# Router logits with the weights held still, and the work between LayerNorm and the first expert gather in another order

## The chip, the cores and the metric

The kernel runs on one core of one Trainium2 chip. The metric is the device time of one execution in microseconds (us). TensorE (PE; its weight loads are listed as PEld) multiplies, VectorE (DVE) and ScalarE (ACT) do elementwise work, GpSimd (POOL) and SyncE (SP) mostly issue DMAs here. TensorE writes into PSUM, eight banks of 128 partitions x 512 float32 numbers; everything else lies in SBUF.

## The reference

Two layers over 304 tokens (272 of a prompt, 32 of a sample). Layer 0 mixes tokens by gated linear attention and latent attention, layer 1 by pooling; each ends in `x = layer_norm(ALPHA * x + out)` and is followed by a mixture of experts and another LayerNorm:

```python
scores = sigmoid(x2 @ router_w)                       # 1024 x 64
biased = scores + router_b
group_score = sum(top_k(biased in 8 groups of 8, 2))  # best 4 groups
idx = top_k(biased inside those groups, 8)
wts = scores[idx] / sum(scores[idx]) * 2.5
routed = sum over idx of wts * (silu(x @ w_gate[e]) * (x @ w_up[e])) @ w_down[e]
shared = (silu(x2 @ sh_gate) * (x2 @ sh_up)) @ sh_down
return layer_norm(ALPHA * x + routed + shared)
```

There are 64 experts with a hidden width of 256; all arithmetic is float32.

## The kernel before

Tokens lie in three tiles of 128, 128 and 64 rows (`ROWS`; 320 columns `T_COLS`, padded to 384). `x` is token-major, `xt` its transpose, eight slices of 128 rows. Each engine runs its own program; semaphores join them. PSUM banks are given out in turn by a fixed list, `bank_uses()` (L211): opening a name waits until the bank's earlier user has been copied out.

Between a mixer and the experts of layer `l` TensorE runs (L1123 to L1150): transposes of x (`xT`, five parts: two for each full tile, one for the last), router products (`lg`, L1130: for each tile, eight products with 128 tokens as weights and the 64 router columns moving), the shared expert's gate and up products (`sg`, `su`, two halves b each, L1134), slot positions (`pos`, L1140: triangular and all-ones matrices times the 0/1 selection), the shared down products (`sd`, L1149), and then `pe_experts` (L756), which reads the number of rounds into a register and gathers the tokens of the first eight experts (L814: eight gathers of five products into banks 2 and 3 in turn). One float32 product is two TensorE instructions; those of the gather (fp32r) are one.

ScalarE makes the LayerNorm's 1/sqrt (`ln_rsqrt`, L1218) for all three tiles, copies `xT` parts 0, 2, 4 into xt (`copy_xt`), takes exp of the logits, makes `xh`, the rounded high part of x (L1346, L1347), and the Silu of sg (L1350). VectorE copies `xT` parts 1 and 3, computes the selection (L1673 to L1705), the normed weights and their split in two parts (L1707 to L1716), the masked selection that `pos` reads (L1717), `sh_h` = Silu(sg) * su (L1723), the slots and the number of rounds (L1724 to L1738), the low parts `xl` of x (L1742, L1743), in layer 0 two identity blocks of `spread` (L1748), the six additions of the shared output to x (L1755), and in `dve_experts` its register load, the weights into `spread` and the one-hot matrix `pick` of the first group (L1364, L1365). Gathered tokens are copied by ScalarE (even slices) and VectorE (odd ones) in turn.

The expert loop then runs over 32 pairs of experts. SyncE (`sp_experts`) loads their weights into two slots; the shared weights lie in the second slot, so its loads wait for `su` and `sd`. In this data one round is enough.

## Time and profile before

| | us |
|---|---|
| median of 3 runs | 1543.93 (1543.57 to 1546.67) |
| profiled execution, its own time | 1544.77 |
| its span in the trace | 1543.0 |
| PE busy | 1454.6 (94%) |
| VectorE busy | 648.0 (42%) |
| ScalarE busy | 364.0 (24%) |

The chain that ended last is TensorE for 90% of the span. All times in the rows below are counted from the span's start. A timeline row has start, duration, engine, line, operation, output <- inputs, the partition and column tile for TensorE, shapes and the number of instructions merged; behind it in brackets the idle time before it and what ended that. In a table of stretches the clock is TensorE's granted clock, 1.00 for 2.4 GHz and 0.50 for 1.2 GHz.

### The profile page before, as it was taken

To read this page: it belongs to the slowest core of one execution; us is meant where nothing else is said; L and a number is where in the kernel's file an instruction comes from. 1 tells how busy PE (TensorE), PEld (TensorE's weight loads), DVE (VectorE), ACT (ScalarE), POOL (GpSimd) and SP (SyncE) were. 2 spreads that over 40 slices of the span, in tenths; PEclk is the share of its full clock that TensorE was granted. 3 is DMA by queue.
4 is the path that set the end of the run, shared out by engine and by line. 5 is a ranking of instruction groups with operands and counts; after the bars stand their busy time and mean duration, and the time that the engine had idled before them with its cause. 6 is when DMAs were issued, how large, how long until landed. Compare 5 with 4: busy or idle time off the path is not lost.

```text
span 1543.0 us, 17906 instructions
## 1 busy us (share of the span) xinstructions
PE 1454.6 (94%) x6555; PEld 772.0 (50%) x6555; DVE 648.0 (42%) x1290; ACT 364.0 (24%) x726; POOL 45.4 (3%) x76
## 2 busy tenths in 40 slices
PE   6998999879999999999999878799999999999995
PEld 4564555555444454454454466454454454444542
DVE  0654532463334334343333466533343343433336
ACT  1441321312122122121221243021221221221213
POOL 4200100100000000000000010000000000000000
PEclk9996557799999999999999986999999999999998
DMA  9102110455998999899899822289989989998970
GB/s 290 64 1 110 42 54 0 160 195 206 391 376 350 420 382 391 367 396 391 350 410 395 346 81 82 109 347 393 374 367 412 374 350 423 379 393 365 394 325 31
DMA packets 63623, 435.31 MB, mean 282 GB/s; under 512 B 4324, under 2 KB 6436, under 8 KB 13537
## 3 DMA queue, kind: packets, MB, share of 16 engines
q1 hardware_dynamic: 60800, 427.18, 69.1%
q0 software_dynamic: 2784, 7.62, 1.7%
q8 instruction: 24, 0.39, 0.1%
q14 instruction: 15, 0.12, 0.0%
HBM read 433.02 MB, written 1.76 MB: 282 GB/s over the span
## 4 chain that ended last, share of the span: by engine, by line
PE 90%; DVE 7%; issue 1%; DMA 1%; ACT 0%; POOL 0%; SPq 0%; DVEq 0%
PE bank L832 29%; PE bank L753 26%; PE bank L786 14%; PE bank L780 12%; PE bank L737 4%; PE bank L842 1%; PE bank L902 1%; DVE sb_ln_st L1444 1%; DVE sb_x L1451 1%; DVE sb_x L1454 1%; PE bank L1008 1%; PE bank L1005 1%; PE bank L1001 1%; DVE sb_x L1755 1%; DVE sb_xl L1423 1%
## 5 line engine op out<-in xcount | busy, mean ns | idle before, releaser
L1378 DVE TENSOR_TENSOR sb_x<-sb_x,bank 128x512 f32<-128x512 f32 (+1 forms) x396 | 242.2, 680 | 118.6 <-PE bank L780 118.6
L786 PE MATMUL bank<-sb_wslot,sb_ht 128*64 128x512 f32 x1024 | 231.0, 593 | 0.0
L832 PE MATMUL bank<-sb_wslot,sb_xg_own 128*64 128x512 f32 x1024 | 226.5, 595 | 1.9 <-DVE sb_xg_own L1370 1.9
L832 PE MATMUL bank<-sb_wslot,sb_xt 128*64 128x512 f32 x1024 | 226.8, 595 | 0.0
L1400 DVE TENSOR_TENSOR sb_hh<-sb_sg,bank 128x256 f32<-128x256 f32 x64 | 27.0, 421 | 367.5 <-ACT sb_sg L1186 367.5
L753 PE MATMUL bank<-sb_pick,sb_xh 128*128 128x512 f32 x432 | 162.9, 406 | 15.6 <-DVE sb_pick L1365 15.6
L1384 DVE SCALAR_TENSOR_TENSOR sb_yl<-bank,sb_gslot,sb_yh 128x512 fp32r<-128x512 f32 x128 | 96.1, 751 | 162.8 <-ACT sb_yh L1168 162.8
L780 PE MATMUL bank<-sb_yh,sb_place 128*128 128x512 f32 x396 | 157.5, 398 | 3.3 <-DVE sb_yl L1384 3.3
L780 PE MATMUL bank<-sb_yl,sb_place 128*128 128x512 f32 x396 | 156.6, 396 | 0.0
L1186 ACT ACTIVATE sb_sg<-bank 128x256 f32<-128x256 f32 x64 | 24.6, 384 | 552.5 <-PE bank L832 552.5
L786 PEld LDWEIGHTS bank<-sb_wslot,sb_ht 128*64 128x64 f32 x1024 | 72.8, 137 | 144.5 <-issue 139.3
L832 PEld LDWEIGHTS bank<-sb_wslot,sb_xg_own 128*64 128x64 f32 x1024 | 71.4, 137 | 140.8 <-issue 139.8
L832 PEld LDWEIGHTS bank<-sb_wslot,sb_xt 128*64 128x64 f32 x1024 | 70.7, 137 | 139.5 <-issue 139.5
L1168 ACT ACTIVATE sb_yh<-bank,sb_gslot 128x512 fp32r<-128x512 f32 x128 | 88.2, 689 | 174.2 <-PE bank L786 174.2
L753 PE MATMUL bank<-sb_pick,sb_xl 128*128 128x512 f32 x288 | 115.0, 399 | 0.0
L753 PEld LDWEIGHTS bank<-sb_pick,sb_xh 128*128 128x128 f32 x432 | 82.6, 191 | 34.3 <-issue 17.3
L780 PEld LDWEIGHTS bank<-sb_yh,sb_place 128*128 128x128 f32 x396 | 74.3, 188 | 27.3 <-DVE sb_x L1378 5.8
L780 PEld LDWEIGHTS bank<-sb_yl,sb_place 128*128 128x128 f32 x396 | 74.5, 188 | 17.2
L1162 ACT ACTIVATE sb_xg_own<-bank 128x512 f32<-128x512 f32 x72 | 43.1, 599 | 97.4 <-PE bank L753 97.4
L753 PEld LDWEIGHTS bank<-sb_pick,sb_xl 128*128 128x128 f32 x288 | 55.3, 192 | 10.3
L1162 ACT ACTIVATE sb_xt<-bank 128x512 f32<-128x512 f32 x64 | 38.4, 599 | 37.7 <-PE bank L753 37.7
L737 PEld LDWEIGHTS bank<-sb_cst,sb_hh 128*128 128x128 f32 x128 | 20.7, 205 | 46.0 <-issue 45.4
(295 smaller groups left out, 1265.5 us busy)
## 6 DMA issues: line engine op xcount, KB each, us to landing
sb_wslot<-in_moe_w_gate_dram SPq DMA_DIRECT2D x64, 2048.0 KB, 8.1
sb_wslot<-in_moe_w_up_dram SPq DMA_DIRECT2D x64, 2048.0 KB, 12.8
sb_wslot<-in_moe_w_down_dram SPq DMA_DIRECT2D x64, 2048.0 KB, 15.1
sb_w_in_hi<-in_w_in_dram SPq DMA_DIRECT2D x2, 2048.0 KB, 22.4
sb_w_in_lo<-in_w_out_dram SPq DMA_DIRECT2D x1, 4096.0 KB, 13.4
sb_w_in_lo<-in_w_in_dram SPq DMA_DIRECT2D x2, 1024.0 KB, 10.9
sb_ln_g<-in_ln_g_dram POOLq DMA_DIRECT2D x4, 512.0 KB, 4.7
sb_ln_b<-in_ln_b_dram POOLq DMA_DIRECT2D x4, 512.0 KB, 6.1
```

What stands on the lines that cost most here:

```text
L737: return pe.transpose(dst, src, ident[0:n, 0:n])
L753: last = pe.matmul(dst, lhs, rhs, start=i == 0, stop=i == len(pairs) - 1)
L780: last = pe.matmul(banks.tile[order[f]][:, :], place[u][:, t * P:(t + 1) * P], part[:, c * 512:(c + 1) * 512], start=h == 0, stop=h == 1)
L786: last = pe.matmul(y_b[c][64 * e:64 * e + 64, :], ht[:, k, 64 * e:64 * e + 64], w_down[u][:, e, k * D + c * 512:k * D + (c + 1) * 512], st ...
L832: last = pe.matmul(gu_b[64 * e:64 * e + 64, :], xgt[b][:, k, sl], w_gu[u][:, :, e, k * FE:(k + 1) * FE], start=k == 0, stop=k == DK_SLICES ...
L842: last = pe.matmul(place_b[:, t * PLACED:(t + 1) * PLACED], pick[b][:, t, q * P:(q + 1) * P], spread[:, b, t, :], start=True, stop=True)
L1162: act.activation(xgt[b][:, kk, :], banks.tile[2 + c][:, :], ACT.Copy).then_inc(s[f"xg_copied{c}"], 1)
L1168: act.activation(yh[:, c * 512:(c + 1) * 512], banks.tile[4 + c][:, :], ACT.Copy, scale=gslot[:, u, :]).then_inc(s[f"yh_ready{c}"], 1)
L1186: act.activation(sg[:, :], gu_b[:, 0:FE], ACT.Silu).then_inc(s["sg_ready"], 1)
L1378: dve.tensor_tensor(dst, dst, banks.tile[order[f]][0:rows, :], ALU.add).then_inc(s["added"], 1)
L1384: dve.scalar_tensor_tensor(out=yl[:, cc], in0=banks.tile[4 + c][:, :], scalar=gslot[:, u, :], in1=yh[:, cc].bitcast(F32), op0=ALU.mult, op ...
L1400: dve.tensor_tensor(hh[:, :], sg[:, :], gu_b[:, FE:2 * FE], ALU.mult).then_inc(s["h_ready"], 1)
```

## The change

The router weights become the weights of TensorE, and the tokens move: the first four slices of K are summed on output partitions 0 to 63, the other four on 64 to 127 (bank `lgT`), first for the 256 tokens of two tiles, then, behind the third tile's transposes, for the last 128. ScalarE copies the 64+64 rows x 384 tokens to `lg_t`, and three products with `two_idents` (two identities of 64 on top of each other) add the halves and bring the logits back token-major. ScalarE copies all five `xT` parts of these stages and all eight gathered slices, splits x tile by tile as each is ready, and writes the identities of `spread`. VectorE subtracts tile by tile, compares all tiles in one operation, writes the masked selection into its own tile `chosen`, and does the normed weights only after the additions. `pos` runs ahead of the last `su`, the register load ahead of `sd`, and `pick` ahead of the additions. The gather waits for banks 2 and 3 alone; the loop waits for the rest (`w_ready`). Cut to its core:

```diff
+    def freed(self, eng, b, name):
+
+n = sum(1 for k in range(self.order.index(name) + 1) if k % 8 == b)
+eng.wait_ge(self.emptied[b], n)
...
-u += [("xT", l + 1, i) for i in range(5)]
-u += [("lg", l)] + [(n, l, b) for b in range(2) for n in ("sg", "su")] + [("pos", l)]
+u += [("xT", l + 1, i) for i in range(4)] + [("lgT", l), ("xT", l + 1, 4), ("lg", l)]
+u += [("sg", l, 0), ("su", l, 0), ("sg", l, 1), ("pos", l), ("su", l, 1)]
...
-sc = rb("sc", [P, TILES, E])
+lg_t = rb("lg_t", [P, T_PAD])
...
-cnt = rb("cnt", [P, E])
+sc = rb("sc", [P, TILES, E])
+sel = rb("sel", [P, TILES, E])
+chosen = rb("chosen", [P, TILES, E])
+tmp = rb("tmp", [P, TILES, E])
...
+    shared_down()
+    pe.wait_ge(s["x_split"], TILES)
+    pe.wait_ge(s["xl_ready"], TILES)
     pe.wait_ge(s["pick_ready"], 1)
+    for b in (2, 3):
+        banks.freed(pe, b, ("sd", l, TILES - 1, 1))
     for kk in range(DK_SLICES):
         if kk > 1:
             pe.wait_ge(s[f"xg_copied{kk % 2}"], kk // 2)
         gather(0, kk)
+    banks.all_copied(pe, ("sd", l, TILES - 1, 1))
+    pe.wait_ge(s["init"], 5)
+    pe.wait_ge(s["w_ready"], 2 - l)
...
+        pe_transpose_x(pe, l + 1, range(4))
...
+        both = banks.open(pe, ("lgT", l))
+
+        def logits(cols):
+            for kk in range(4):
+                for h in range(2):
+                    last = pe.matmul(both[64 * h:64 * h + 64, cols], w_rt[:, 4 * h + kk, :], xt[:, 4 * h + kk, cols],
+                                     start=kk == 0, stop=kk == 3)
+            return last
+
+        for i in range(4):
+            banks.copied(pe, ("xT", l + 1, i))
+        logits(slice(0, 2 * P))
+        pe_transpose_x(pe, l + 1, (4,))
+        banks.copied(pe, ("xT", l + 1, 4))
+        logits(slice(2 * P, T_PAD)).then_inc(banks.fill_sem(("lgT", l)), 1)
+        banks.copied(pe, ("lgT", l))
         ps = banks.open(pe, ("lg", l))
         for t in range(TILES):
-            last = accumulate(pe, ps[:, t * E:(t + 1) * E], [(xt[:, k, t * P:(t + 1) * P], w_rt[:, k, :]) for k in range(8)])
+            last = pe.matmul(ps[:, t * E:(t + 1) * E], lg_t[:, t * P:(t + 1) * P], const("two_idents"), start=True, stop=True)
         last.then_inc(banks.fill_sem(("lg", l)), 1)
...
+        def shared(name, w, b):
+            stage((name, l, b), lambda ps: accumulate(pe, ps[:, 0:T_COLS], [
+                (w[:, k, b::2], xt[:, k, 0:T_COLS]) for k in range(8)]))
...
+        shared("sg", sh_gate, 0)
+        shared("su", sh_up, 0)
+        shared("sg", sh_gate, 1)

         pe.wait_ge(s["sel_ready"], 1)
...
+            accumulate(pe, ps[:, t * E:(t + 1) * E], [(const("ones"), chosen[:, i, :]) for i in range(t)] +
...
+        shared("su", sh_up, 1)
+
+        def shared_down():
+            for b in range(2):
+                banks.copied(pe, ("su", l, b))
+            token_products("sd", l, lambda k, tc: sh_h[:, k, tc], sh_down, 2)
+
+        pe_experts(pe, l, shared_down)
...
-    for m in range(QUAD):
-        copy_xg(0, 2 * m, m + 1)
+    for kk in range(DK_SLICES):
+        copy_xg(0, kk, kk // 2 + 1)
...
-    ln_rsqrt(0)
...
+        def split_high(t):
+            rows = ROWS[t]
+            act.wait_ge(x_ready, 6 * l + t + 1)
+            act.activation(xh[0:rows, t, :, :], x[0:rows, t, :].rearrange("p (f k) -> p k f", k=DK_SLICES), ACT.Copy)\
+               .then_inc(s["x_split"], 1)
+
+        ln_rsqrt(2 * l, (0, 1))
+        copy_xt(l + 1, (0, 1))
...
+        split_high(0)
+        ln_rsqrt(2 * l, (2,))
+        copy_xt(l + 1, (2, 3))
+        split_high(1)
+        copy_xt(l + 1, (4,))
+        copy(lg_t[:, :], ("lgT", l), lambda ps: ps[:, 0:T_PAD])
...
-        act.activation(xh[:, 0:2, :, :], by_k(x[:, 0:2, :]), ACT.Copy)
-        act.activation(xh[0:64, 2, :, :], x[0:64, 2, :].rearrange("p (f k) -> p k f", k=DK_SLICES), ACT.Copy)\
-           .then_inc(s["x_split"], 1)
+        split_high(2)
+        if l == 0:
+            act.wait_ge(s["init"], 5)
+            for b in range(2):
+                act.activation(spread[:, b, 0:2, 0:P], bc(ident, 1, 2), ACT.Copy)
+                ins = act.activation(spread[0:64, b, 2, 0:P], ident[0:64, :], ACT.Copy)
+            ins.then_inc(s["w_ready"], 1)
...
-    def copy_xg(b, kk, n):
-        dve.wait_ge(s["xg_done1"], n)
-        dve.tensor_copy(xgt[b][:, kk, :], banks.tile[3][:, :]).then_inc(s["xg_copied1"], 1)
+        spread_weights(b, c0)
+        pick_slots(b, c0)

...
-    pick_group(0, slice(0, GROUP_E))
-    for m in range(QUAD):
-        copy_xg(0, 2 * m + 1, m + 1)
...
-        copy_xt(l + 1)
...
+        def split_low(t):
+            rows = ROWS[t]
+            dst = xh[64:128, 2, :, :] if t == 2 else xl[:, t, :, :]
+            dve.wait_ge(s["x_split"], t + 1)
+            dve.tensor_tensor(dst, x[0:rows, t, :].rearrange("p (f k) -> p k f", k=DK_SLICES),
+                              xh[0:rows, t, :, :].bitcast(F32), ALU.subtract).then_inc(s["xl_ready"], 1)
+
+        def spread_weights(b, c0):
+            return dve.tensor_copy(spread[:, b, :, P:].rearrange("p t (e h) -> p t e h", h=2), w_split[:, :, c0, :])
+
+        def pick_slots(b, c0):
+            iota = bc(bc(const("iota"), 1, GROUP_E), 1, TILES)
+            dve.tensor_tensor(pick[b][:, :, :].rearrange("p t (e n) -> p t e n", e=GROUP_E), iota,
+                              bc(pos_x[:, :, c0], 3, SLOTS), ALU.is_equal).then_inc(s["pick_ready"], 1)
+
+        split_low(0)
+        split_low(1)
...
-        for t in range(TILES):
-            other, own = bc(gs[:, t, :], 1, NG), bc(gs[:, t, :], 2, NG)
-            tt(cmp1[:, t, :, :], other, own, ALU.is_gt)
-            tt(cmp2[:, t, :, :], other, own, ALU.is_equal)
-            tt(cmp2[:, t, :, :], cmp2[:, t, :, :], const("lower_group").rearrange("p (g n) -> p g n", g=NG), ALU.mult)
+        other, own = bc(gs[:, :, :], 2, NG), bc(gs[:, :, :], 3, NG)
+        lower = bc(const("lower_group").rearrange("p (g n) -> p g n", g=NG), 1, TILES)
+        tt(cmp1[:, :, :, :], other, own, ALU.is_gt)
+        tt(cmp2[:, :, :, :], other, own, ALU.is_equal)
+        tt(cmp2[:, :, :, :], cmp2[:, :, :, :], lower, ALU.mult)
...
-        tt(tmp[:, :, :], sc[:, :, :], sel[:, :, :], ALU.mult)
-        step(dve.tensor_reduce(wsum[:, :], tmp[:, :, :], AX.X, ALU.add))
...
-        tt(sel[:, :, :], sel[:, :, :], valid, ALU.mult, s["sel_ready"])
...
+        tt(chosen[:, :, :], sel[:, :, :], valid, ALU.mult, s["sel_ready"])
+
+        def gate_hidden(b):
...
             dve.tensor_tensor(sh_h[:, b, :], sh_sg[:, b, :], ps[:, 0:T_COLS], ALU.mult).then_inc(banks.empty_sem(n), 1)
+
+        gate_hidden(0)
+        split_low(2)
...
-        dve.wait_ge(s["x_split"], 1)
-        for t in range(2):
...
-           ALU.subtract, s["x_split"])
...
-            dve.wait_ge(s["init"], 5)
-            for b in range(2):
-                step(dve.tensor_copy(spread[:, b, 0:2, 0:P], bc(ident, 1, 2)))
-                step(dve.tensor_copy(spread[0:64, b, 2, 0:P], ident[0:64, :]))
+        gate_hidden(1)
+        pick_slots(0, slice(0, GROUP_E))
...
-        dve_experts(dve, l, step)
+        tt(tmp[:, :, :], sc[:, :, :], sel[:, :, :], ALU.mult)
+        step(dve.tensor_reduce(wsum[:, :], tmp[:, :, :], AX.X, ALU.add))
...
+        step(dve.tensor_copy(w_split[:, :, E:, :], w_split[:, :, 0:GROUP_E, :]))
+        if l == 0:
+            dve.wait_ge(s["init"], 5)
+        spread_weights(0, slice(0, GROUP_E)).then_inc(s["w_ready"], 1)
+        dve_experts(dve, l, spread_weights, pick_slots)
```

## Rows read from the trace of the kernel before

**Rows 1.** Page, part 2: TensorE's busy tenths in 40 slices of 38.6 us.

```profile
PE   6998999879999999999999878799999999999995
```

**Rows 2.** TensorE's longest waits, 355:905 (us, times, longest); then one stretch of the loop.

```profile
PE bank L780 <- DVE sb_yl L1384: 1.7, 1, 1.7
...
387.00:404.00 17.00, 17.00 (x79) 8.13 (x77) 5.82 (x11) 3.62 (x7) 0.00 (x0) 1.00 0.96 386
```

**Rows 3.** Timeline, layer 0, TensorE: start us, us, engine, line, operation [idle before].

```profile
291.71 1.14 PE L737 MATMUL bank<-sb_cst,sb_x 64*128 64x64 f32 x8 [0.66 <-DVE sb_x L1454]
293.95 10.48 PE L753 MATMUL bank<-sb_w_rt,sb_xt 128*128 128x64 f32 x48 [1.10 <-POOL sb_yl L723]
304.22 19.57 PE L753 MATMUL bank<-sb_xt,sb_wslot 128*128 128x320 f32 x64
...
325.58 7.08 PE L753 MATMUL bank<-sb_wslot,sb_xg_own 128*128 128x512 f32 x16
...
343.04 0.76 PE L753 MATMUL bank<-sb_pick,sb_xh 128*128 128x512 f32 x1 [8.50 <-DVE sb_pick L1365]
...
354.95 7.09 PE L832 MATMUL bank<-sb_wslot,sb_xg_own 128*64 128x512 f32 x32 [0.98 <-DVE sb_xg_own L1370]
```

**Rows 4.** The same timeline in layer 1.

```profile
937.42 10.47 PE L753 MATMUL bank<-sb_w_rt,sb_xt 128*128 128x64 f32 x48 [1.10 <-ACT sb_xt L1207]
947.69 18.70 PE L753 MATMUL bank<-sb_xt,sb_wslot 128*128 128x320 f32 x64
...
984.24 0.77 PE L753 MATMUL bank<-sb_pick,sb_xh 128*128 128x512 f32 x1 [7.11 <-DVE sb_pick L1365]
```

**Rows 5.** Stretches: us, busy (x) of PE, PEld, DVE, ACT, POOL, clock, DMA, GB/s.

```profile
243.40:247.50 4.10, 4.10 (x17) 1.67 (x16) 1.97 (x5) 0.00 (x0) 0.00 (x0) 0.55 0.00 0
248.00:276.00 28.00, 27.52 (x64) 12.08 (x64) 3.75 (x7) 1.78 (x3) 0.00 (x0) 1.00 0.00 1
304.20:308.50 4.30, 4.30 (x10) 2.83 (x10) 3.21 (x9) 3.95 (x2) 0.00 (x0) 0.50 1.01 426
345.70:354.00 8.30, 8.27 (x35) 6.33 (x33) 2.08 (x3) 2.24 (x4) 0.00 (x0) 0.98 0.00 0
984.30:987.50 3.20, 3.20 (x8) 2.52 (x9) 0.00 (x0) 0.60 (x1) 0.00 (x0) 0.50 0.00 0
```

**Rows 6.** Timeline, mixer stage: TensorE's pairs on 64 output columns each.

```profile
68.59 3.67 PE L926 MATMUL bank<-sb_w_in_hi,sb_xt 128*64 128x256 f32 x32
...
243.36 4.19 PE L1084 MATMUL bank<-sb_w_in_hi,sb_w_uv 128*64 128x320 f32 x16
```

**Rows 7.** Timeline, layer 0, ScalarE.

```profile
286.47 1.28 ACT L1215 ACT_TABLE_LOAD   x1 [4.60 <-DVE sb_ln_mv L1445]
...
292.89 0.60 ACT L1207 ACTIVATE sb_xt<-bank 128x512 f32<-128x512 f32 x1 [2.05 <-PE bank L737]
...
304.77 3.92 ACT L1346 ACTIVATE sb_xh<-sb_x 128x2048 fp32r<-128x2048 f32 x1
```

**Rows 8.** Timeline, layer 0, VectorE.

```profile
305.01 0.26 DVE L1426 TENSOR_SCALAR sb_sc<-sb_sc 128x192 f32<-128x192 f32 x1 [12.03 <-ACT sb_sc L1344]
...
316.31 0.36 DVE L1423 TENSOR_TENSOR sb_tmp<-sb_sc,sb_sel 128x192 f32<-128x192 f32 x1
...
319.31 0.36 DVE L1423 TENSOR_TENSOR sb_sel<-sb_sel,sb_cst 128x192 f32<-128x192 f32 x1
...
323.83 0.49 DVE L1723 TENSOR_TENSOR sb_xg_own<-sb_xg_own,bank 128x320 f32<-128x320 f32 x1 [3.64 <-PE bank L753]
325.78 0.36 DVE L1727 TENSOR_SCALAR sb_pos_x<-bank 128x192 f32<-128x192 f32 x1 [1.47 <-PE bank L753]
...
328.49 4.07 DVE L1423 TENSOR_TENSOR sb_xl<-sb_x,sb_xh 128x1024 fp32r<-128x1024 f32 x2
...
341.04 0.19 DVE L1364 CAST sb_spread<-sb_w_split 128x48 fp32r<-128x48 f32 x1 [0.96 <-DVE sb_x L1755]
341.15 1.74 DVE L1365 TENSOR_TENSOR sb_pick<-sb_cst,sb_pos_x 128x1536 fp32r<-128x1536 f32 x1
```

More of the change, by code:

```diff
@@ L107, in constants @@
     put(cst, CST, "lower_group", np.tile((g[None, :] < g[:, None]).reshape(1, -1), (P, 1)))
+    put(cst, CST, "two_idents", np.tile(np.eye(E), (2, 1)))
     mix = np.zeros((P, MIX_W), f)
@@ L444, in build @@
         mr = rb("mr", [P, TILES, E])
-        sel = rb("sel", [P, TILES, E])
-        tmp = rb("tmp", [P, TILES, E])
         mx8 = rb("mx8", [P, TILES, 8])
@@ L737, in transpose, with pe_transpose_x @@
             return pe.transpose(dst, src, ident[0:n, 0:n])
-        def pe_transpose_x(pe, n):
-            for i in range(5):
+        def pe_transpose_x(pe, n, parts):
+            for i in parts:
                 t, k0, nk = xt_part(i)
@@ L759, in pe_experts @@
             xg_b, y_b = banks.tile[2:4], banks.tile[4:6]
-            banks.all_copied(pe, ("sd", l, TILES - 1, 1))
             def gather(b, kk):
@@ L868, in _ @@
             pe.wait_ge(x_in, 16 * 5)
-            pe_transpose_x(pe, 0)
+            pe_transpose_x(pe, 0, range(5))
             def stage(name, pairs_of):
@@ L1141, in _ @@
                 for t in range(TILES):
-                    accumulate(pe, ps[:, t * E:(t + 1) * E], [(const("ones"), sel[:, i, :]) for i in range(t)] +
-                               [(const("before"), sel[:, t, :])])
-                accumulate(pe, ps[:, TILES * E:(TILES + 1) * E], [(const("ones"), sel[:, i, :]) for i in range(TILES)])\
+                    accumulate(pe, ps[:, t * E:(t + 1) * E], [(const("ones"), chosen[:, i, :]) for i in range(t)] +
+                               [(const("before"), chosen[:, t, :])])
+                accumulate(pe, ps[:, TILES * E:(TILES + 1) * E], [(const("ones"), chosen[:, i, :]) for i in range(TILES)])\
                     .then_inc(banks.fill_sem(("pos", l)), 1)
-                for b in range(2):
-                    banks.copied(pe, ("su", l, b))
-                token_products("sd", l, lambda k, tc: sh_h[:, k, tc], sh_down, 2)
-                pe_experts(pe, l)
+                shared("su", sh_up, 1)
[4 more added lines that the diff above has]
+                pe_experts(pe, l, shared_down)
         def act_experts(act, l):
@@ L1207, in copy, with copy_xt @@
                 act.activation(dst, src(ps) if src else ps, ACT.Copy).then_inc(banks.empty_sem(name), 1)
-            def copy_xt(n):
-                for i in range(0, 5, 2):
+            def copy_xt(n, parts):
+                for i in parts:
                     t, k0, nk = xt_part(i)
@@ L1216, in rsqrt, with ln_rsqrt @@
                 step(act.activation(dst, dst, ACT.Exp, scale=-0.5), sem)
-            def ln_rsqrt(n):
-                for t in range(TILES):
+            def ln_rsqrt(n, tiles=range(TILES)):
+                for t in tiles:
                     rows = ROWS[t]
@@ L1222, in ln_rsqrt @@
                     rsqrt(ln_rs[0:rows, t:t + 1], ln_mv[0:rows, t, 1:2], 1.0, eps[0:rows, 0:1], rs_ready)
-            copy_xt(0)
+            copy_xt(0, range(0, 5, 2))
             for j in range(2, 4):
@@ L1353, in _, with dve_experts @@
                 ln_rsqrt(2 * l + 1)
-        def dve_experts(dve, l, step):
+        def dve_experts(dve, l, spread_weights, pick_slots):
             s = L[l]
@@ L1687, in _ @@
                 tt(gs[:, :, :], g_a[:, :, :, 0], g_b[:, :, :, 0], ALU.add)
-                for t in range(TILES):
-                    other, own = bc(gs[:, t, :], 1, NG), bc(gs[:, t, :], 2, NG)
-                    tt(cmp1[:, t, :, :], other, own, ALU.is_gt)
-                    tt(cmp2[:, t, :, :], other, own, ALU.is_equal)
-                    tt(cmp2[:, t, :, :], cmp2[:, t, :, :], const("lower_group").rearrange("p (g n) -> p g n", g=NG), ALU.mult)
+                other, own = bc(gs[:, :, :], 2, NG), bc(gs[:, :, :], 3, NG)
[3 more added lines that the diff above has]
+                tt(cmp2[:, :, :, :], cmp2[:, :, :, :], lower, ALU.mult)
                 tt(cmp1[:, :, :, :], cmp1[:, :, :, :], cmp2[:, :, :, :], ALU.add)
@@ L1728, in _ @@
                 step.banked(dve.tensor_copy(cnt[:, :], ps[:, TILES * E:(TILES + 1) * E]), banks, n)
-                tt(pos_x[:, :, 0:E], pos_x[:, :, 0:E], sel[:, :, :], ALU.mult)
+                tt(pos_x[:, :, 0:E], pos_x[:, :, 0:E], chosen[:, :, :], ALU.mult)
                 ts(pos_x[:, :, 0:E], pos_x[:, :, 0:E], -1.0, None, ALU.add)
@@ L1738, in _ @@
                 ts(n_rounds[:, :], cmax[:, :], 1.0, None, ALU.add, None, s["rounds_ready"])
-                dve.wait_ge(s["x_split"], 1)
-                for t in range(2):
-                    tt(xl[:, t, :, :], x[:, t, :].rearrange("p (f k) -> p k f", k=DK_SLICES), xh[:, t, :, :].bitcast(F32), ALU.subtract)
-                tt(xh[64:128, 2, :, :], x[0:64, 2, :].rearrange("p (f k) -> p k f", k=DK_SLICES), xh[0:64, 2, :, :].bitcast(F32),
-                   ALU.subtract, s["x_split"])
-                if l == 0:
-                    dve.wait_ge(s["init"], 5)
-                    for b in range(2):
-                        step(dve.tensor_copy(spread[:, b, 0:2, 0:P], bc(ident, 1, 2)))
-                        step(dve.tensor_copy(spread[0:64, b, 2, 0:P], ident[0:64, :]))
+                gate_hidden(1)
+                pick_slots(0, slice(0, GROUP_E))
                 for t in range(TILES):
```

36 lines of the change are left out of this document (10 added, 26 removed).

## Prediction

> **What bounds the kernel now.** I read the page's slices first: TensorE is busy nine tenths or more nearly throughout, with dips in slices 8 and 9 and again in 23 to 26 [rows 1]. Each expert loop is TensorE's own. In the list of TensorE's waits from 355 to 905 us the loop's own longest is 1.7 us, for yl, and none is for a DMA; a stretch of 17 us shows 17.00 us busy at a clock share of 1.00 while the DMAs moved 386 GB/s [rows 2]. So a microsecond saved before a loop should shift the whole loop. The two routing stretches, where the dips are, I read as a timeline of TensorE: 289 to 355 us in layer 0 [rows 3] and 937 to 984 us in layer 1 [rows 4]. Three losses are to be seen. The router's products take 10.48 us as 48 instructions of 64 columns, each with 128 columns of weights, 0.218 us apiece. TensorE idles 8.50 us (layer 1: 7.11) between the shared down products and the first gather. And it pays for low clock after each: 1.2 instead of 2.4 GHz, share 0.50, for the first 4.3 us of the shared products and the first 3.2 us of layer 1's gather [rows 5].
>
> **Router products.** Of 24 logical products of 128 token weights, 16 become ones that hold 64 router columns and stream 256 or 128 tokens, two halves of K at once on two column halves; then three fold the halves by a doubled identity. What TensorE does with such pairs is in two rows: 32 instructions of 256 columns in 3.67 us at full clock (0.115 each), 16 of 320 columns in 4.19 us at low clock (0.262 each, half of what 320 columns cost alone) [rows 6]. At low clock 16 instructions of 256 columns then take 16 x 0.262 x 256/320 = 3.4 us. No pair of 128 columns is in the trace; it lies between that rate (1.7 us) and the present 0.218 per load (3.5 us); I take 1.7, since a load is now 64 columns, not 128. The fold's six instructions are like the present ones: 6 x 0.218 = 1.3.
> In layer 0 the second tile's transposes end 0.66 before 291.71 [rows 3]; its ACT copies (0.60 each, row 292.89 [rows 7]) end near 291.8, and TensorE follows 0.4 later, as 0.46 separates today's last copy and 293.95. From 292.2: 3.4, the third tile's transposes 1.14, hand-over and copy 1.1, second part 1.7, hand-over and copy of lg_t 1.0, fold 1.3. That is 301.9, against 304.22: 2.3 us saved. Layer 1 has the same spacing; 2.4.
> ACT takes over all five xt copies and the splits. An x tile costs 1.96 us (half of 3.92) [rows 7]. split_high(0) sits ahead of the third tile's rsqrt, which starts today at 286.47; copies from about 283.8 and the split end at 287.1, so rsqrt ends 0.6 us later, about when VectorE asks. I count 0, at most 0.6. split_high(1) (291.8 to 293.8) is over before the third tile's bank fills at 296.8: cost 0. If TensorE's first part were as short as 1 us, it would be in the way.
>
> **Selection.** From the first operation on sc at 305.01 to the end of sel at 316.31 are 11.3 us; `chosen` adds 0.4 [rows 8]. The nine comparisons of a tile each become three larger ones, which only shortens this. Cover is now three shared stages, 48 instructions of 0.27 us (0.43 for 512 columns, 27.52 us for 64, times 320/512 [rows 5]), 13.0 us at full clock. The chain starts 0.5 behind the fold and needs at most 11.7, so slack is 0.8 us or more. The two split_low ahead of it (2.03 each, half of 4.07 [rows 8]) run from 291.7 to about 296, before the logits exist. The ten weight operations (3.0 us, 316.31 to 319.31) leave this chain for the time behind the adds, under the gather of 9.4 us: cost 0, and what passes 9 us there would be exposed before the loop.
>
> **Order of pos and su.** pos now comes ahead of the last shared stage, so the slot chain (325.78 to 328.49, 2.7 us [rows 8]) runs under 4.3 us of products. The price: the shared down products now wait directly for the last su, its multiplication and two hand-overs, near 0.9 us, where today pos lies between. TensorE's load of the number of rounds stands there too; VectorE's such load shows as 0.96 idle before 341.04 [rows 8]. In parallel it costs nothing, behind the wait another 1.0. Bounds 0.9 to 1.9; I take 1.4 in each layer.
>
> **The gap before the gather.** Today VectorE does after n_rounds: 4.07 of split, 2.0 more, the identity casts (layer 0), six adds, the register load, 0.19 and 1.74 for slots, ending at 342.9 [rows 8]. After, splits are done early, casts go to ACT (behind sc, before the first Silu, nobody waits), and pick_slots (1.74) begins some 0.5 us after the last su, 9 us before the shared down products end. By the bank order those of tile 0 take banks 2 and 3, which the gather needs; they are added 5 us before it. So the whole gap goes: 8.5 and 7.1 us. What is late next is TensorE itself. The gather then follows dense work and runs at full clock: 40 instructions x 0.236 (8.27 us for 35 [rows 5]) = 9.4 instead of 10.9 (343.04 to 353.97), 1.5 saved; layer 1, with 3.2 us at low clock, 1.6. Now all eight copies are ACT's, 0.6 every 1.17 us: no wait; the last is 0.1 shorter than VectorE's.
>
> **Clock in the shared products.** They took 19.57 and 18.70 us; 64 x 0.27 is 17.3. In the present trace the clock stayed at 1.2 GHz through all of the router's 10.48 us and rose 4.3 us into the dense products behind them [rows 5]. After the change 3.4 us of dense pair products come before. The 4.1 us of pair products at 243.4 show a share of 0.55, and the 512-column ones right behind them 1.00 [rows 5]. I take it as full when the shared products begin: 2.2 and 1.4 saved. If it is not, these fall away (+3.6); if it is full from the second part of the logits on, another 1.9 per layer goes.
>
> **Sum.** Layer 0: -2.3 + 1.4 - 8.5 - 1.5 - 0.1 - 2.2 = -13.2. Layer 1: -2.4 + 1.4 - 7.1 - 1.6 - 0.1 - 1.4 = -11.2. Together -24.4 from the profiled execution's own 1544.8: 1520.4. The median of the runs lies 0.8 lower, so **1519.6 us**. With the clock late 1523.2, with it early 1515.8; hand-overs and 128-column loads add 1.0 and 3.6 at most.
> SP's order is untouched. The load of the second slot's gate, issued behind the shared down products, has 10 us less lead before the first expert pair, but serves the second pair, 16 us later.
>
> **Rivals.**
> *The halves run one after the other.* Both halves use all 128 rows, and their weights might not load beside the other's product. Then the logits cost 3.4 + 1.7 us more in each layer: 1519.6 + 10.2 = 1529.8. The pair rows speak against it [rows 6]. The Trainium skill ("TensorE: Matmul & The Clock Gate", Part 3, "The mechanism") says that a weight load overlaps a product in flight only when their row groups differ, which is not so here; by that rule the time would be this rival's. The trace disagrees: pairs on all 128 rows came every 0.115 us for 256 columns. Chance 4%.
> *VectorE or ACT becomes the bound.* If the selection is late by 2 us (slack 0.8) or pick_slots and hand-overs are, TensorE waits and part of the clock is lost: +3 us a layer, 1525.6. For it: ten small links in a row. Against it: slack at each, as above. Chance 15%.
> *The gain is swallowed by the weights.* If the loop ran at the DMAs' pace, an earlier start would move nothing: 1544. Against it, no wait of TensorE on a DMA [rows 2]. Chance 2%.
> *Slower: the clock does not come back.* The place is from the fold to the end of the gather. The logits now have four short stops of TensorE. If these kept it at 1.2 GHz through shared, pos, down and gather (17.3 + 2.1 + 9.0 + 9.4 = 37.8 us at full clock), each layer pays 37.8 in place of what I saved as clock (3.7 and 3.0): 1519.6 + 75.6 + 6.7 = 1602. It decides from about 12 us of low-clock work extra per layer, so a return later than 24 us after the first shared product. Against it: the clock rose within 4.3 us each time dense work began [rows 5]. Chance 3%.
>
> **Chances.** Forecast with its clock variants (1514 to 1524) 76%, late selection 15%, serial halves 4%, swallowed 2%, slower 3%. The range 1513 to 1528 takes in the variants and late selection, without the last three. A measurement here tells about 0.2%, 3 us, from no change. Faster 0.95, same 0.02, slower 0.03.
>
> **What would show it.** Logits as 32 + 6 instructions from transposes to the first shared product in under 11 us; no idle over 1 us between shared down and gather; gather at 0.234 us an instruction from its first; first expert product 13 and then 24 us earlier. TensorE waiting for `chosen`, or an expert loop longer than before, would make the prediction wrong.

## The result, and the profile after

The changed kernel takes 1519.28 us (median of 4 runs, 1516.69 to 1521.64), the kernel before 1544.4 beside it. The ratio is 0.9831, 95% interval 0.9817 to 0.9844. The forecast was 1519.6. The profiled execution has a span of 1519.9 us.

TensorE's timeline in layer 0 is to be laid beside [rows 3]; columns are as there.

```profile
291.22 1.97 PE L746 MATMUL bank<-sb_cst,sb_x 128*128 128x128 f32 x8 [4.80 <-DVE sb_x L1494]
293.96 3.47 PE L1145 MATMUL bank<-sb_xt,sb_w_rt 128*64 128x256 f32 x16 [0.78 <-ACT sb_xt L1242]
297.36 1.09 PE L746 MATMUL bank<-sb_cst,sb_x 64*128 64x64 f32 x8
299.14 1.09 PE L1145 MATMUL bank<-sb_xt,sb_w_rt 128*64 128x128 f32 x16 [0.69 <-ACT sb_xt L1242]
300.83 0.88 PE L1158 MATMUL bank<-sb_cst,sb_lg_t 128*128 128x64 f32 x6 [0.59 <-ACT sb_lg_t L1242]
301.55 13.14 PE L762 MATMUL bank<-sb_xt,sb_wslot 128*128 128x320 f32 x48
314.53 2.12 PE L762 MATMUL bank<-sb_chosen,sb_cst 128*128 128x64 f32 x18
316.48 4.53 PE L762 MATMUL bank<-sb_xt,sb_wslot 128*128 128x320 f32 x16
321.69 7.10 PE L762 MATMUL bank<-sb_wslot,sb_xg_own 128*128 128x512 f32 x16 [0.68 <-issue]
328.73 1.94 PE L903 MATMUL bank<-sb_wslot,sb_xg_own 128*64 128x512 f32 x8
330.60 0.50 PE L762 MATMUL bank<-sb_pick,sb_xh 128*128 128x512 f32 x1
```

Four things are to be seen. The router's products are now the two L1145 rows and the fold (L1158), 38 instructions instead of 48. `pos` (314.53) stands inside the shared stages. The first gather (330.60) starts behind the last shared down product with no idle time in its bracket, where [rows 3] has 8.50. And its first product takes 0.50 us, not 0.76: the clock is up. In layer 1 the same rows are:

```profile
922.81 3.68 PE L1145 MATMUL bank<-sb_xt,sb_w_rt 128*64 128x256 f32 x16 [0.78 <-ACT sb_xt L1242]
926.43 1.14 PE L746 MATMUL bank<-sb_cst,sb_x 64*128 64x64 f32 x8
928.25 1.98 PE L1145 MATMUL bank<-sb_xt,sb_w_rt 128*64 128x128 f32 x16 [0.69 <-ACT sb_xt L1242]
930.82 1.54 PE L1158 MATMUL bank<-sb_cst,sb_lg_t 128*128 128x64 f32 x6 [0.59 <-ACT sb_lg_t L1242]
932.15 14.74 PE L762 MATMUL bank<-sb_xt,sb_wslot 128*128 128x320 f32 x48
...
953.90 7.11 PE L762 MATMUL bank<-sb_wslot,sb_xg_own 128*128 128x512 f32 x16 [0.68 <-issue]
...
973.26 7.09 PE L846 MATMUL bank<-sb_wslot,sb_xg_own 128*64 128x512 f32 x32 [0.87 <-ACT sb_xg_own L1197]
```

The second part of the logits takes 1.98 us here and 1.09 in layer 0, the fold 1.54 and 0.88. That is the granted clock, 1.00 in layer 0's second part and 0.50 in layer 1 from both parts of the logits until 3 us into the shared products. In the changed kernel's table of stretches, with columns as in [rows 5], the clock is the third figure from the end of a row:

```profile
293.90:297.40 3.50, 3.44 (x17) 1.98 (x17) 3.50 (x2) 1.91 (x1) 3.50 (x6) 0.55 0.72 220
299.10:300.20 1.10, 1.06 (x16) 0.85 (x16) 0.00 (x0) 0.00 (x0) 0.00 (x0) 1.00 1.04 432
922.80:926.40 3.60, 3.59 (x16) 1.90 (x16) 3.60 (x2) 1.83 (x1) 1.05 (x2) 0.50 0.61 146
932.10:935.20 3.10, 3.10 (x8) 2.12 (x8) 2.23 (x4) 2.78 (x3) 0.00 (x0) 0.50 0.00 0
935.20:946.00 10.80, 10.80 (x41) 7.79 (x41) 9.73 (x32) 1.21 (x2) 0.00 (x0) 0.99 0.00 0
```

The starts of the same instructions in the timelines of all profiles cut the execution into stretches, in us. They are: (a) first transposes to first shared product, (b) to the first shared down product, (c) to the gather, (d) to the first expert product. For before, layer 0, they are 283.14 (the transposes of tile 0), then the starts in [rows 3].

| kernel | start to (a) | layer 0: a, b, c, d | loop | LayerNorm, pooling | layer 1: a, b, c, d | rest |
|---|---|---|---|---|---|---|
| before | 283.1 | 21.08, 21.36, 17.46, 11.91 | 530.6 | 40.0 | 22.13, 20.49, 16.06, 12.12 | 546.6 |
| changed | 285.3 | 16.29, 20.14, 8.91, 10.48 | 530.7 | 41.3 | 19.09, 21.75, 8.90, 10.46 | 546.6 |

Layer 0's four fell from 71.81 to 55.82, by 16.0 us, layer 1's from 70.80 to 60.20, by 10.6. The loops did not move. The two parts that the change does not touch were 2.1 and 1.3 us longer in this one execution. Of the 2.1, 1.8 are in the kernel's first projections, the same 64 instructions in 19.28 us here and 17.46 before. Over the 14 profiles of this study the start varied from 280.4 to 285.3 and the pooling stretch from 39.7 to 43.3. So 26.6 less 3.5 (2.1, 1.3 and 0.1 in the loop) are the 23.1 us between the two spans.

### The profile page after: what moved, and what is told of

Its sections match the earlier page's. It is cut to its first block, busy times and chain, and to the rows that moved or that the text cites. A ratio compares the mean times of both kernels' runs of the same rounds, so it can differ in the third digit from the quotient of the medians.

```text
span 1519.9 us, 17857 instructions
## 1 busy us (share of the span) xinstructions
PE 1445.7 (95%) x6535; PEld 759.0 (50%) x6535; DVE 637.1 (42%) x1262; ACT 372.6 (25%) x746; POOL 45.4 (3%) x76
## 4 chain that ended last, share of the span: by engine, by line
PE 93%; DVE 5%; issue 1%; ACT 1%; DMA 1%; SPq 0%; DVEq 0%
PE bank L846 29%; PE bank L762 25%; PE bank L794 15%; PE bank L788 12%; PE bank L746 4%; PE bank L856 1%; PE bank L916 1%; DVE sb_ln_st L1484 1%; PE bank L1022 1%; PE bank L903 1%; DVE sb_x L1491 1%; DVE sb_x L1494 1%; PE bank L1145 1%; PE bank L1019 1%; PE bank L1015 1%
## 5 line engine op out<-in xcount | busy, mean ns | idle before, releaser
L1197 ACT ACTIVATE sb_xg_own<-bank 128x512 f32<-128x512 f32 x80 | 47.9, 599 | 78.3 <-PE bank L762 78.3
```

The costliest lines, as they stand in the source:

```text
L1197: act.activation(xgt[b][:, kk, :], banks.tile[2 + c][:, :], ACT.Copy).then_inc(s[f"xg_copied{c}"], 1)
```

## The experiments

All are edits of the changed kernel but the first; the diffs are cut. Times are medians, with the ratio to the kernel before on the same chip.

**1. The router products alone, in the kernel before.**

```diff
-pe_transpose_x(pe, l + 1)
+pe_transpose_x(pe, l + 1, range(4))
...
+both = banks.open(pe, ("lgT", l))
...
+logits(slice(0, 2 * P))
+pe_transpose_x(pe, l + 1, (4,))
...
+logits(slice(2 * P, T_PAD)).then_inc(banks.fill_sem(("lgT", l)), 1)
...
 for t in range(TILES):
-    last = accumulate(pe, ps[:, t * E:(t + 1) * E], [(xt[:, k, t * P:(t + 1) * P], w_rt[:, k, :]) for k in range(8)])
+    last = pe.matmul(ps[:, t * E:(t + 1) * E], lg_t[:, t * P:(t + 1) * P], const("two_idents"), start=True, stop=True)
```

> The kernel before with the router products of the change alone (logits through lgT and lg_t; everything else in the old order). My theory: the two traces give a stretch from the first transposes to the first shared product that is 4.8 us shorter in layer 0 (21.08 to 16.29) and 3.0 in layer 1 (22.13 to 19.09), and nothing behind it in the old order is waiting for something else, so about 1537 us, 7 to 8 below the kernel before. Rival: in the old order VectorE's chain, not TensorE, sets the gather's start, and the saving turns into a longer idle before the gather (over 11 us instead of 8.5), so 1544.

1542.73 us, 0.9981 (0.9968 to 0.9993). The stretches: a, b, c, d are 17.90, 19.24, 17.46, 12.63 and 18.83, 20.94, 16.07, 12.37, together 7.2 us under before. Stretch (c) is unchanged at 17.46, so the idle ahead of the gather did not grow and the rival falls. Stretch (a) fell by 3.2 and 3.3 where I had 4.8 and 3.0; in layer 0 another 2.1 came in (b), and (d) took 0.7 and 0.3 more. Of the whole, where I had 7 to 8, only 3.0 us of the medians are seen; in its profile 3.2 us went to the LayerNorm and pooling stretch (43.2), which the edit leaves alone. The profiles of late_pick, late_split_pick and pos_last below have 43.0 to 43.3 there too, so that stretch is not this kernel's own; why the median of ten runs keeps only 3.0 is open.

TensorE's timeline of router_only, the two parts of the logits in layer 0:

```profile
293.14 3.68 PE L1133 MATMUL bank<-sb_xt,sb_w_rt 128*64 128x256 f32 x16 [2.07 <-POOL sb_yh L725]
...
298.58 1.09 PE L1133 MATMUL bank<-sb_xt,sb_w_rt 128*64 128x128 f32 x16 [0.69 <-ACT sb_xt L1223]
```

The first row waits 2.07 us, in the changed kernel 0.78: in the old order VectorE copies two of the transposed parts, and only behind its LayerNorm. The copies on ScalarE are worth 1.3 us a layer to the new router products.

**2. The old router products in the changed kernel.**

```diff
-pe_transpose_x(pe, l + 1, range(4))
+pe_transpose_x(pe, l + 1, range(5))
...
-logits(slice(0, 2 * P))
...
-last = pe.matmul(ps[:, t * E:(t + 1) * E], lg_t[:, t * P:(t + 1) * P], const("two_idents"), start=True, stop=True)
+last = accumulate(pe, ps[:, t * E:(t + 1) * E], [(xt[:, k, t * P:(t + 1) * P], w_rt[:, k, :]) for k in range(8)])
```

> The changed kernel with the old router products (24 products with tokens as weights, after all five transposes). My theory: it loses what the new ones gave, 7 to 8 us: about 1527. The low clock comes back into the first 2 to 4 us of the shared products. Rival, by which most of the gain comes from the later clock and the router products themselves give little: 1521 to 1523.

1532.95 us, 0.9911 (0.9883 to 0.9939), worse than I expected by 6. The eight stretches sum to 127.95 against 116.02, 11.9 more: 5.5 and 3.7 in (a), 1.8 and 1.0 in (b), nothing in (c) and (d).

TensorE's timeline of router_undone, the router's products and the first shared ones in layer 0:

```profile
295.73 10.48 PE L762 MATMUL bank<-sb_w_rt,sb_xt 128*128 128x64 f32 x48 [1.79 <-ACT sb_xt L1228]
306.00 14.89 PE L762 MATMUL bank<-sb_xt,sb_wslot 128*128 128x320 f32 x48
```

The products are the 10.48 us of [rows 3]. They wait 1.79 us, not 1.10, since ScalarE now has the second tile's split (292.67 to 294.77) ahead of the last copy. The edit also takes out ScalarE's copy to `lg_t`. So the two halves of the change help each other: router alone -7.2, the rest alone -14.7, both -26.6. Of the 4.7 between, the rows give 2.6 to the earlier copies (experiment 1) and 1.4 to this wait. These are single profiles: with the second profile of the changed kernel (experiment 9) both together are -29.8, so this division is good to some 3 us only.

**3 to 5. What closed the gap ahead of the gather.** The late split:

```diff
-split_high(0)
...
-split_high(1)
...
-split_high(2)
+for t in range(TILES):
+    split_high(t)
...
-split_low(0)
-split_low(1)
...
-split_low(2)
...
 gate_hidden(1)
+for t in range(TILES):
+    split_low(t)
+dve.wait_ge(s["xl_ready"], TILES)
 pick_slots(0, slice(0, GROUP_E))
```

> The changed kernel with x split late: ScalarE makes the high parts of all tiles behind the exp, VectorE the low parts (6.1 us) behind the last gating and ahead of the slots. My theory: from the last gating VectorE has 9 us under the shared down products; 6.1 + 1.75 + two additions of 0.7 are 9.3, so the gather starts about 0.5 us later in each layer, 1520.3 us in all. Rival: the early splitting is what closed the gap, so 6.1 us come back per layer, 1531.5.

The late one-hot matrix:

```diff
-pick_slots(0, slice(0, GROUP_E))
 for t in range(TILES):
...
+pick_slots(0, slice(0, GROUP_E))
 tt(tmp[:, :, :], sc[:, :, :], sel[:, :, :], ALU.mult)
```

> The changed kernel with the slots' one-hot matrix made behind the six additions, as before the change. My theory: the additions end 1.6 us after the last shared down product and the matrix takes 1.75, so TensorE idles about 3.5 us in each layer: 1526.3, one or two more if the clock falls in the idle. Rival: the matrix is hidden wherever it stands, 1519.3.

Both at once:

> The changed kernel with x split late and the one-hot matrix behind the additions, both at once. My theory: the 6.1 us of splitting run under the shared down products, and only the last additions and the matrix are behind them, so it is like the late matrix alone: 12.5 us from the first shared down product to the gather, and gather at low clock, about 10 us over the changed kernel. Rival: the two add up, 6.1 us more per layer, 18.6 us in that stretch.

| | us | ratio | (c) by layer | (d) by layer |
|---|---|---|---|---|
| late_split | 1517.84 | 0.983 (0.981 to 0.985) | 9.04, 9.04 | 10.45, 10.44 |
| late_pick | 1530.69 | 0.9904 (0.9887 to 0.992) | 12.48, 12.49 | 11.98, 11.89 |
| late_split_pick | 1534.93, one run | | 12.48, 12.48 | 11.99, 11.92 |

The early splitting is worth 0.13 us a layer in the changed kernel: done late, it runs under the shared down products. The place of the one-hot matrix is worth 3.6 us a layer in (c), and 1.5 in (d), since the gather behind the idle starts at low clock. I had put 3.5 and one or two in all. The two do not add up: with both, (c) is the same.

TensorE's timeline of late_pick, the first product of layer 0's gather with the idle ahead of it:

```profile
331.87 0.47 PE L762 MATMUL bank<-sb_pick,sb_xh 128*128 128x512 f32 x1 [3.51 <-issue]
```

VectorE's timeline of late_split_pick, from the splitting to the one-hot matrix:

```profile
322.83 3.92 DVE L1712 TENSOR_TENSOR sb_xl<-sb_x,sb_xh 128x1024 fp32r<-128x1024 f32 x2
326.78 2.00 DVE L1712 TENSOR_TENSOR sb_xh<-sb_x,sb_xh 64x1024 fp32r<-64x1024 f32 x1
328.82 2.85 DVE L1795 SCALAR_TENSOR_TENSOR sb_x<-sb_x,bank 128x512 f32<-128x512 f32 x4
332.08 1.41 DVE L1795 SCALAR_TENSOR_TENSOR sb_x<-sb_x,bank 64x512 f32<-64x512 f32 x2 [0.41 <-PE bank L903]
333.52 1.76 DVE L1720 TENSOR_TENSOR sb_pick<-sb_cst,sb_pos_x 128x1536 fp32r<-128x1536 f32 x1
```

In VectorE's rows the three subtractions (322.83, 326.78) end before the last shared down product fills its bank; the last two additions (332.08) still have to wait 0.41 for it. Before the change (c) was 17.46. The 5.0 us from there to 12.48 are what VectorE no longer does between the first shared down product and the matrix: the slot chain, 2.7 by [rows 8], the register load, 0.96, and the identity casts, 1.15 (334.63 to 335.79 in the kernel before). Layer 1 has no identity casts, and there the difference is 3.6. That sum is an argument from the rows; no run took these out one at a time. The rows also show that the 0.13 is not what the splits cost before the change. There the 6.1 us of splitting (328.49 to 334.6) stood in the same unbroken chain of VectorE ahead of the additions. Taking them alone out of it would, as an estimate, leave 17.46 - 6.1 = 11.4, less than the 12.48 at which the last additions and the matrix stand, so it would have won the same 5.0. No run tried that. In late_split_pick (a) and (b) of layer 0 were 0.65 and 2.58 longer than in the changed kernel, which the idle does not explain: the second part of the logits took 1.09 us at clock 1.00, the fold behind it 1.54, and the shared products ran at 0.50 until 305 us.

**6 and 7. The place of pos, and of the register load.** pos behind all four shared stages:

```diff
 shared("sg", sh_gate, 1)
+shared("su", sh_up, 1)
 pe.wait_ge(s["sel_ready"], 1)
...
-shared("su", sh_up, 1)
...
 split_low(2)
+gate_hidden(1)
...
-gate_hidden(1)
```

> The changed kernel with the slot positions behind all four shared stages again; the register load still ahead of the shared down products. My theory: the slot chain of VectorE (2.7 us) and the load (0.7 to 1.0) are then no longer under a shared stage, so from the first shared product to the first shared down product it takes about 22.9 us at full clock instead of 20.14, 2.7 more in each layer. Rival: the place of pos is indifferent, because the products wait for the gating either way: 20.1.

The same, and the load behind the shared down products:

```diff
-pe.wait_ge(s["rounds_ready"], 1)
-rounds = pe.value_load(n_rounds[0:1, 0:1], min_val=1, max_val=MAX_ROUNDS)
 shared_down()
+pe.wait_ge(s["rounds_ready"], 1)
+rounds = pe.value_load(n_rounds[0:1, 0:1], min_val=1, max_val=MAX_ROUNDS)
```

> The changed kernel with pos behind all four shared stages and the register load behind the shared down products. My theory: pos covers the gating again, so the first shared down product comes 19.2 us after the first shared product instead of 20.14 (at full clock), 0.9 less per layer, and if TensorE loads the register while products are still queued, 8.9 us later the gather starts as now: 1517.5. Rival: the load can only run when the products are done, 0.7 to 1.0 us of idle ahead of the gather, and nothing is won: 1519.3.

pos_last: one run, 1527.69 us; (b) is 23.15 and 22.95, about 2.9 more than 20.15, as expected, and (c) 10.4 instead of 8.9, because the products behind the stop start at low clock. The timeline of pos_last, VectorE and TensorE in layer 0:

```profile
322.46 0.15 DVE L1465 TENSOR_SCALAR sb_n_rounds<-sb_cmax 128x1 int32<-128x1 f32 x1
322.65 1.76 DVE L1720 TENSOR_TENSOR sb_pick<-sb_cst,sb_pos_x 128x1536 fp32r<-128x1536 f32 x1
...
323.65 2.90 PE L762 MATMUL bank<-sb_wslot,sb_xg_own 128*128 128x512 f32 x3 [3.74 <-issue]
```

VectorE has the number of rounds at 322.61; TensorE's next product starts 1.04 us later. That is the price of the load, with the hand-over to it, where nothing covers it.

pos_load_last: 1512.79 us, 0.9799 (0.978 to 0.9818), 4.7 under what I expected. (b) is 19.25 and 19.24 instead of 20.15, 0.9 less in each layer, (c) 8.88: the load in front of the gather costs nothing.

TensorE's timeline of pos_load_last, from the first shared down product to the gather:

```profile
318.49 7.08 PE L762 MATMUL bank<-sb_wslot,sb_xg_own 128*128 128x512 f32 x16
325.50 1.94 PE L903 MATMUL bank<-sb_wslot,sb_xg_own 128*64 128x512 f32 x8
327.37 0.50 PE L762 MATMUL bank<-sb_pick,sb_xh 128*128 128x512 f32 x1
```

There is no idle in the first row's bracket, where the changed kernel has 0.68 at 321.69. So moving pos ahead of the last shared stage was not a gain in itself: it only makes room for the slot chain that the load, standing ahead of the shared down products, waits for. What the shared down products of the changed kernel wait for is the gating. VectorE's timeline of the changed kernel, layer 0, the number of rounds and the last gating:

```profile
319.20 0.15 DVE L1466 TENSOR_SCALAR sb_n_rounds<-sb_cmax 128x1 int32<-128x1 f32 x1
321.11 0.49 DVE L1770 TENSOR_TENSOR sb_xg_own<-sb_xg_own,bank 128x320 f32<-128x320 f32 x1 [1.75 <-PE bank L762]
```

The number is there at 319.35, over 2 us ahead of TensorE's product at 321.69; the gating ends at 321.60. By these rows moving the load alone would give nothing, and with the load moved the old order of pos is better; the load moved with pos in its new place was not run. The rows show 1.8 us of the difference to the changed kernel; the rest is not in these stretches and is not explained, and the intervals of the two ratios overlap.

**8. The halves of K on one column half.**

```diff
-last = pe.matmul(both[64 * h:64 * h + 64, cols], w_rt[:, 4 * h + kk, :], xt[:, 4 * h + kk, cols],
-                 start=kk == 0, stop=kk == 3)
+last = pe.matmul(both[0:64, cols], w_rt[:, 4 * h + kk, :], xt[:, 4 * h + kk, cols],
+                 start=kk + h == 0, stop=kk + h == 4)
...
-    last = pe.matmul(ps[:, t * E:(t + 1) * E], lg_t[:, t * P:(t + 1) * P], const("two_idents"), start=True, stop=True)
+    last = pe.matmul(ps[:, t * E:(t + 1) * E], lg_t[0:64, t * P:(t + 1) * P], const("two_idents")[0:64, :], start=True, stop=True)
...
-copy(lg_t[:, :], ("lgT", l), lambda ps: ps[:, 0:T_PAD])
+copy(lg_t[0:64, :], ("lgT", l), lambda ps: ps[0:64, 0:T_PAD])
```

> The changed kernel with both halves of K on the same 64 output columns, so that no two products of the logits run side by side. My theory: the 16 instructions of 256 tokens take twice as long, 6.9 us at low clock instead of 3.47, those of 128 tokens 2.1 instead of 1.09 at full clock; from the first transposes to the first shared product 19.5 to 21 us in layer 0 instead of 16.29. Rival, the rule that a weight load is only hidden where the rows differ: the pairs gain nothing and the time stays at 16.3.

One run, 1521.81 us. (a) is 18.83 in layer 0 and 20.71 in layer 1.

TensorE's timeline of one_column, the two parts of the logits in layer 0:

```profile
293.11 5.08 PE L1145 MATMUL bank<-sb_xt,sb_w_rt 128*64 128x256 f32 x16 [0.78 <-ACT sb_xt L1242]
...
299.90 1.96 PE L1145 MATMUL bank<-sb_xt,sb_w_rt 128*64 128x128 f32 x16 [0.69 <-ACT sb_xt L1242]
```

The second part in the table of stretches, columns as in [rows 5]:

```profile
299.90:301.90 2.00, 1.96 (x16) 1.72 (x16) 0.00 (x0) 0.00 (x1) 0.00 (x0) 1.00 1.02 399
```

At full clock the 16 instructions of 128 tokens take 1.96 us, side by side 1.09. Those of 256 take 5.08 instead of 3.47 and not 6.9, as the clock rose inside them; that is why (a) is 2.5 over the changed kernel's in layer 0 and not the 3.2 or more that I expected. The rival, that pairs gain nothing, falls. In the row above the weight loads show as busy for 1.72 of the 2.00 us and the products for 1.96, so the loads ran under products here too. By this, what the pairs gain is two products at a time and not hidden loads.

**9 to 12. The clock.** The changed kernel once more:

> The changed kernel itself once more, beside the others on one chip. It should come within 1516 to 1522 us; how its stretches differ from the first profile shows what the clock's timing alone does: both theories expect the loops at 530.6 and 546.6 us, and 1 to 3 us of play in the stages with low clock.

Products that nobody reads, in the LayerNorm waits. This is added work and its results are unused; one product of `warm` is `pe.matmul(bank[:, :], ident, cst[:, 0:512])`:

```diff
+fb, fn = banks.at[("lgT", l)]
+pe.wait_ge(banks.emptied[fb], fn)
+if l:
+    warm(pe, fb, 4)
+pe_transpose_x(pe, l + 1, range(2))
+warm(pe, fb, 5)
-pe_transpose_x(pe, l + 1, range(4))
+pe_transpose_x(pe, l + 1, range(2, 4))
```

> The changed kernel with products of constants that nobody reads (five of 512 columns, 4.3 us, between the first two tiles' transposes; in layer 1 four more ahead of the first) in TensorE's waits for LayerNorm. Added work, no result. My theory: the clock then stays at 2.4 GHz, the logits' first part takes 1.8 us instead of 3.5, and from the first transposes to the first shared product it is about 14.3 us in both layers instead of 16.3 and 19.1, the shared products without a slow start: 8 us less, 1511. Rival: the clock falls in the transposes and copies all the same, or the added work delays the transposes: 1519 or more.

The same filling with the old router products:

> The same filling with the old router products. My theory: the router products themselves run at 2.4 GHz then, 48 instructions at 0.11 to 0.2 us, so 5 to 9 us instead of 10.5, and the new form is worth less: from the first transposes to the first shared product 16 to 19 us. Rival: the router's products let the clock fall by themselves, as 64 columns for each 128 of weights; then 21 us as before.

And everywhere, with the order of pos_load_last: the filling above, four such products while the first tokens are loaded, and eight ahead of layer 1's pooling stage:

> pos and the register load last as in pos_load_last, and unread products in all of TensorE's long waits: while the first tokens are loaded, and in the LayerNorms. Added work, no result. My theory: the 8 us of the filled LayerNorms, and 1 to 5 more from the first projections and layer 1's pooling stage; 1512.8 less 6 to 10 gives 1503 to 1507, with less play between runs. Rival, by which the clock returns as late as before: 1512.

| | us | ratio | (a) by layer | (b) by layer |
|---|---|---|---|---|
| changed_again | 1516.46 | 0.9825 (0.9808 to 0.9843) | 16.14, 17.59 | 20.16, 20.15 |
| filled_ln | 1514.46 | 0.9801 (0.9786 to 0.9816) | 14.28, 17.31 | 20.15, 22.75 |
| router_undone_filled | 1531.44 | 0.992 (0.9892 to 0.9947) | 21.34, 22.14 | 22.74, 22.07 |
| filled_all | 1509.31 | 0.9779 (0.9758 to 0.9799) | 14.29, 15.66 | 19.25, 20.35 |

The same code, run again, has layer 1 in 57.10 us instead of 60.20. TensorE's timeline of changed_again, layer 1, the second part of the logits:

```profile
926.23 1.09 PE L1145 MATMUL bank<-sb_xt,sb_w_rt 128*64 128x128 f32 x16 [0.69 <-ACT sb_xt L1242]
```

It takes 1.09 us against 1.98 in the first profile: the clock was up from there on. Filling took layer 0's (a) to 14.28, as expected; in layer 1 it did not work. The table of stretches of filled_ln there: the last filling, the second tile's transposes, the first part of the logits, the third tile's transposes, the second part, the fold, the first shared products:

```profile
912.90:917.30 4.40, 4.40 (x12) 1.72 (x10) 4.23 (x6) 4.37 (x5) 0.00 (x0) 1.00 0.62 201
918.90:920.10 1.20, 1.16 (x8) 0.97 (x8) 1.20 (x1) 0.38 (x1) 0.00 (x0) 1.00 0.97 410
920.90:924.50 3.60, 3.55 (x17) 1.98 (x17) 3.57 (x3) 1.87 (x1) 1.05 (x2) 0.54 0.37 115
924.50:926.20 1.70, 1.02 (x8) 0.88 (x8) 0.98 (x1) 0.60 (x1) 0.00 (x0) 1.00 0.95 340
926.20:927.90 1.70, 1.11 (x17) 0.87 (x17) 0.00 (x0) 0.49 (x1) 0.00 (x0) 0.92 0.11 43
927.90:929.30 1.40, 1.40 (x7) 1.40 (x7) 0.00 (x0) 0.00 (x0) 0.00 (x0) 0.50 0.00 0
929.30:931.80 2.50, 2.50 (x6) 1.72 (x6) 1.80 (x3) 2.31 (x3) 0.00 (x0) 0.50 0.00 0
```

The filling ran at 1.00, and 3.5 us behind its end (917.37, five products, ten instructions, from 912.91 in 4.46 us) the logits' first part is at 0.54; in the fold the clock fell again, and 2.5 us of shared products at 0.50 followed. So of 8 us expected, 2 are seen in the medians, and the intervals of the two kernels overlap. The eight stretches of filled_ln sum to 113.23, against 116.02 and 112.78 in the two profiles of the changed kernel, so the rows show no gain beyond the play. The old router products show more of it. The table of stretches of router_undone_filled, layer 0: the second and third tile's transposes, the wait behind them, and the router's products in two stretches:

```profile
286.40:287.50 1.10, 1.10 (x8) 0.92 (x8) 1.10 (x1) 1.06 (x3) 0.00 (x0) 1.00 0.00 0
289.00:290.10 1.10, 1.10 (x8) 0.93 (x8) 1.10 (x1) 1.10 (x1) 1.10 (x2) 0.91 0.62 74
290.10:291.40 1.30, 0.01 (x1) 0.00 (x0) 1.30 (x2) 0.92 (x2) 1.30 (x3) 0.50 0.66 164
291.80:298.00 6.20, 6.20 (x31) 6.20 (x30) 1.17 (x1) 0.00 (x0) 1.19 (x3) 0.50 1.01 418
298.00:302.00 4.00, 4.00 (x20) 4.00 (x20) 0.00 (x0) 0.01 (x1) 0.00 (x0) 0.50 1.01 377
```

The clock was up in the transposes and down in the wait of 1.37 us behind them, and 10.47 us of the router's products without a stop did not bring it back, although TensorE shows as busy throughout (6.20 of 6.20, 4.00 of 4.00). In the changed kernel's layer 0 the clock stood at 0.55 in the first part of the logits and at 1.00 in the second; in layer 1 of the same execution it was 0.50 in both and came back 3 us into the shared products. So filling ahead of the old products changes nothing for them: the rival's time came true, but its reason, that these products let the clock fall, is not shown, as the clock had fallen in the wait ahead of them. What they would take if the clock were still up at their first was not tried. filled_all is the fastest kernel of the study in its median, 35 us under before, but above the 1503 to 1507 that I expected; over pos_load_last its gain is not clear of the intervals.

## Why the prediction was right

The total was right to 0.3 us, by parts of which several were less exact. Measured values are differences of the stretches above.

- **The gap.** Forecast -8.5 and -7.1, measured -8.55 and -7.16 in (c). The claim that TensorE itself is late next is shown: no idle ahead of 330.60. How it divides among its reasons is shown only in part: experiments 3 to 5 put 3.6 us a layer on the matrix's place. The remaining 5.0 and 3.6 are read from VectorE's chain, where the early splits, the slot chain, the register load and the casts could each stand in for one another; once the others are out of the chain, the splits' place is worth 0.13.
- **The gather.** Forecast -1.6 and -1.7 with the last copy, measured -1.43 and -1.66 in (d).
- **The router's logits.** Forecast -2.3 and -2.4, measured -4.79 and -3.04 in (a). The pairs at low clock were as worked out (3.4; measured 3.47 and 3.68). The second part was 1.98 at low clock in layer 1 against my 1.7, inside its bounds. Mis-sized were the hand-overs, idle 0.78, 0.69 and 0.59 where I had 1.15, 1.1 and 1.0 with the copies, and the clock, which was up from 297 on in layer 0: 1.09 for 1.7 and 0.88 for 1.3.
- **Order of pos and su.** Forecast +1.4, with 0.9 and 1.9 as bounds. At full clock (b) is 20.15 against 19.24 in pos_load_last: 0.9, the lower bound. The register load is hidden in parallel, as the rows under experiment 7 show. The idle is 0.68, which is the gating and its hand-overs.
- **Clock in the shared products.** Forecast -2.2 and -1.4. Layer 0 had it. Layer 1 did not: shared products at 0.50 for 3.1 us, so (b) rose by 1.26 where I had 0.0. In changed_again layer 1 had it too. This term came out differently in two executions of the same kernel and should have stood as a spread, not as a value; "I take it as full" was the weakest step.
- **Selection and ScalarE.** No wait of TensorE on `chosen` shows: pos starts right behind the third shared stage. The split ahead of the third tile's rsqrt cost nothing to be seen: the third tile's transposes (297.36) start without idle time ahead of them.
- **The loops.** 530.6 and 546.6 in both, so what is saved ahead of them arrives whole.

Layer 0 came 2.8 us better than my sum, layer 1 0.6 worse, and 3.5 us went elsewhere in this execution. That the total fits so closely is partly chance: the same kernel measured again had a median of 1516.46, 3.1 us under the forecast.

The rule of the Trainium skill ("TensorE: Matmul & The Clock Gate", Part 3, "The mechanism") that a weight load overlaps only a product on other rows does not describe these pairs: on the same 128 rows they ran 1.8 times as fast as one column half alone (1.96 to 1.09 us). Nor does the trace bear it out without pairs: in [rows 5] weight loads are busy for 2.83 of the 4.30 us from 304.20, in which products on all 128 rows are busy throughout. The measurement decides.
